# Start offsets of the split activations in four feed-forward stages

## The reference

```
h = rms_norm(x, g)                       # 256 x 1024
gate, up = split(h @ w13)                # 1024 x 5632, D_FF = 2816
x = x + 0.5 * rms_norm(silu(gate) * up @ w2)     # 2816 x 1024
```

## Time and profile before

| what | value |
|---|---|
| device time, 3 runs | 2018.49, 2027.36, 2029.08 us |
| median | 2027.36 us |
| profiled execution, own time | 2015.41 us |
| its span | 2013.2 us |
| granted TensorE clock in it | 0.998 of full speed |
| PE busy | 1977.8 us (98%), 15408 matmuls |
| PEld busy | 1843.3 us (92%) |
| DVE, ACT, POOL busy | 1342.0, 1082.5, 51.9 us |
| HBM read | 353.65 MB, 176 GB/s over the span |

### The profile page before, as it was taken

One profiled execution on the slowest core, in us unless ns is written; L12 is line 12 of the kernel. 1 busy time (PEld: TensorE's weight loads), 2 busy tenths in 40 slices (PEclk: granted clock), 3 DMA queues, 4 the chain that ended last, 5 costly groups with the idle time before them and its releaser, 6 DMA issues.

```text
span 2013.2 us, 37724 instructions
## 1 busy us (share of the span) xinstructions
PE 1977.8 (98%) x15408; PEld 1843.3 (92%) x15408; DVE 1342.0 (67%) x1866; ACT 1082.5 (54%) x1698; POOL 51.9 (3%) x47
## 2 busy tenths in 40 slices
PE   7999999999999999999999999999999999999998
PEld 7989989999899989899988998999899989888997
DVE  6776766787566657866867555655477678756554
ACT  5846555555454454555556444644454565645443
POOL 0021000000000000000100000000000001000000
PEclk9999999999999999999999999999999999999999
DMA  7521455566566647543553655565655535545553
GB/s 274 168 85 66 144 189 168 198 202 199 176 218 194 199 168 232 184 137 128 208 199 137 230 192 196 187 211 190 198 193 184 177 109 189 181 159 168 189 190 123
DMA packets 98729, 359.30 MB, mean 178 GB/s; under 512 B 11192, under 2 KB 11512, under 8 KB 98296
## 3 DMA queue, kind: packets, MB, share of 16 engines
q1 hardware_dynamic: 98560, 356.90, 53.6%
HBM read 353.65 MB, written 1.05 MB: 176 GB/s over the span
## 4 chain that ended last, share of the span: by engine, by line
PE 92%; DVE 4%; ACT 3%; issue 1%; DMA 0%; DVEq 0%; SPq 0%; ACTq 0%
PE ps L1040 17%; PE ps L1042 17%; PE ps L1041 17%; PE ps L1027 8%; PE ps L1114 7%; PE ps L1116 7%; PE ps L1115 7%; PE ps L1196 2%; PE ps L1081 2%; PE ps L1083 2%; PE ps L1082 2%; PE ps L1197 2%; PE ps L1203 2%; DVE wlo L1719 1%; ACT whi L2463 1%
## 5 line engine op out<-in xcount | busy, mean ns | idle before, releaser
L1719 DVE TENSOR_TENSOR wlo<-raw,whi 128x1024 fp32r<-128x1024 f32 x635 | 773.6, 1228 | 458.1 <-ACT whi L2463 456.0
L2463 ACT ACTIVATE whi<-raw 128x1024 fp32r<-128x1024 f32 x635 | 664.5, 1056 | 351.3 <-PE ps L1116 154.4
L1040 PE MATMUL ps<-H,whi 128*128 128x256 f32 x2608 | 732.9, 281 | 2.4 <-DVE wlo L1719 1.6
L1042 PE MATMUL ps<-H,wlo 128*128 128x256 f32 x2608 | 724.6, 278 | 0.0
L1041 PE MATMUL ps<-L,whi 128*128 128x256 f32 x2608 | 724.1, 278 | 0.0
L1040 PEld LDWEIGHTS ps<-H,whi 128*128 128x128 f32 x2608 | 490.0, 188 | 8.3 <-issue 4.0
L1041 PEld LDWEIGHTS ps<-L,whi 128*128 128x128 f32 x2608 | 490.4, 188 | 0.6
L1042 PEld LDWEIGHTS ps<-H,wlo 128*128 128x128 f32 x2608 | 490.3, 188 | 0.0
L1114 PE MATMUL ps<-whi,HH 128*128 128x512 f32 x440 | 171.2, 389 | 0.0
L1115 PE MATMUL ps<-whi,HL 128*128 128x512 f32 x440 | 171.2, 389 | 0.0
L1116 PE MATMUL ps<-wlo,HH 128*128 128x512 f32 x440 | 171.2, 389 | 0.0
(11 more groups left out here) (441 smaller groups left out, 2936.4 us busy)
## 6 DMA issues: line engine op xcount, KB each, us to landing
raw<-in_ws SPq DMA_DIRECT2D x635, 512.0 KB, 3.7
prow<-in_rows SPq DMA_DIRECT2D x11, 512.0 KB, 5.3
row<-in_rows SPq DMA_DIRECT2D x9, 512.0 KB, 6.4
mema<-in_memT SPq DMA_DIRECT2D x4, 512.0 KB, 4.9
mema<-in_mem2T SPq DMA_DIRECT2D x4, 512.0 KB, 6.0
memb<-in_mem2T SPq DMA_DIRECT2D x4, 512.0 KB, 5.7
DT<-in_dec SPq DMA_DIRECT2D x2, 768.0 KB, 6.5
X<-in_x SPq DMA_DIRECT2D x1, 1024.0 KB, 10.9
```

Of the source, the lines that this page charges most:

```text
L1040: e.matmul(o, h, hs[k], start=first and k == 0, stop=False, skip_group_check=True)
L1042: mm = e.matmul(o, lo, hs[k], start=False, stop=last and end, skip_group_check=True)
L1719: e.tensor_tensor(m.wlo[:, n % SPL, :], r, h.bitcast(F32), SUB).then_inc(*c.lo.done(n))
L2463: e.activation(m.whi[:, n % SPL, :], m.raw[:, n % RAW, :], ACT.Copy).then_inc(*c.hi.done(n))
```

## The change

The table `BEGIN` gets other numbers for four stages. `f` goes from (64, 64) to (128, 128), `("a", 0)` to (192, 192), `("b", 0)` to (128, 192), and `("a", 1)` to (192, 128), the first of a pair for `H` and the second for `L`. `("b", 1)` and all others keep theirs. The views still fit in the stores (192 is under the slack of 256). Instructions, their order, their shapes and the waits stay as they are; what differs is the start address in the operands that name `H` or `L` in those stages: written in the junction before, read in `head` and `fin`.

```diff
-BEGIN = {..., "f": (64, 64), ("a", 0): (64, 64), ..., ("b", 0): (64, 64), ("a", 1): (64, 64), ..., ("b", 1): (64, 64)}
+BEGIN = {..., "f": (128, 128), ("a", 0): (192, 192), ..., ("b", 0): (128, 192), ("a", 1): (192, 128), ..., ("b", 1): (64, 64)}
```

More of the change, by code:

```diff
@@ L21 @@
 SPREAD = (16, 40, 58, 82.5)
-BEGIN = {"x0": (64, 64), "mix": (0, 0), "c": (64, 64), "f": (64, 64), ("a", 0): (64, 64), ("m", 0): (64, 64), ("o", 0): (0, 0), ("c", 0): (64, 64), ("b", 0): (64, 64), ("a", 1): (64, 64), ("m", 1): (64, 64), ("o", 1): (0, 0), ("c", 1): (64, 64), ("b", 1): (64, 64)}
+BEGIN = {"x0": (64, 64), "mix": (0, 0), "c": (64, 64), "f": (128, 128), ("a", 0): (192, 192), ("m", 0): (64, 64), ("o", 0): (0, 0), ("c", 0): (64, 64), ("b", 0): (128, 192), ("a", 1): (192, 128), ("m", 1): (64, 64), ("o", 1): (0, 0), ("c", 1): (64, 64), ("b", 1): (64, 64)}
 HIDDEN = {"f": (0, 0), ("a", 0): (0, 0), ("b", 0): (0, 0), ("a", 1): (0, 0), ("b", 1): (0, 0)}
```

## The result

The changed kernel takes 2038.02 us (median of 5 runs, 2035.26 to 2040.09), the kernel before 2027.36 (5 runs, 2018.49 to 2030.23). The ratio reported for these runs is 1.0077, with a 95% interval of 1.0049 to 1.0106; the quotient of the two medians is 1.0053. So slower is clear, and the size is known only as 0.5 to 1%. The forecast was no change, 2026 us; the measured time lies inside the range of 2013 to 2045, but just above the 2037.5 up to which it would have passed for no change. The profiled execution took 2035.79 us over a span of 2033.6, which is 20.4 us more span than the profiled execution of before.

The account below looks back on a forecast made before the run. TensorE's matmul stream was taken to bound the kernel. The profiled 2015.41 us plus 2 x 4.7 = 9.4 us for drawn slow stages gave 2024.8; between that and the median of 2027.36 it took 2026, range 2013 to 2045.

Parts of the forecast that it names:

- What bounds the kernel: Whole kernel: TensorE busy 98% of the span, so a change in matmul pace counts in full; VectorE and ScalarE have slack.
- Two paces at one offset: Feed-forward stages with `H` and `L` at 64: 113.3 or 117.7 ns a matmul, each held for a whole stage.
- Writing `H` and `L` costs nothing: Junctions: writing at other offsets taken as 0, at most 1 us either way; `H` writes outside 573 to 603 ns would refute.
- the floor: Matmuls of the four stages: 113.3 ns, the lowest distance seen; no gain below it expected.
- The bound of 28 us of gain: Four stages, 4224 matmuls: most that could be gained if new offsets removed every bubble, 6.7 ns each, giving 1987 us.
- The forecast case: Four changed stages draw their pace anew, chance one half each: 9.4 us over all fast, 2024.8, taken as 2026; chance 0.35.
- The rival of the slow lock: Four changed stages: reads meet in every matmul at 128 or 192, 120.0 ns, 28.2 us more, 2043.6 us; chance 0.3.
- Its nearest row: Mixers' 512-column matmuls with stationary operand at 64, distance 192: 233.3 ns, 6.6 more than at 0, so 192 read as slow.
- The test I named in advance: `fin` of four stages: if `f` and `("a", 0)` differ and the mixed stages lie between by thirds, offset rules, not draw.
- The sign that I had set for the forecast being wrong: `fin` of the four stages: forecast wrong if all four show a pace not seen in the profile before.
- The rule of the Trainium skill: TensorE has two independent SBUF read ports, so the four stages run at 109.2 ns at every offset; change worth 0.

Follow-up runs that it names:

- the second shifted kernel: Kernel before with `whi` and `wlo` 64 bytes further on, `H` and `L` both at 64, 128, 192, 0, 64 in the five feed-forwards: 2045.26 us, one run.

## Why the prediction was wrong, point by point

*What bounds the kernel* held: 19.2 of the 20.4 us are matmul pace in three of the four stages, with TensorE never idle there and the other engines unchanged.

*Two paces at one offset* held, and with them goes most of the spread of the runs. *Writing `H` and `L` costs nothing* held: its sign, durations of `H` outside 573 to 603 ns, was passed by 1 and 3 ns (572, 606) with the median unchanged at 592. So did the floor: no feed-forward in 14 profiles went under 113.3 ns. The bound of 28 us of gain stayed untouched.

*The forecast case failed in "neither offset ruling it out".* 192 doesn't rule the fast pace out, 128 does. At 128 the stage locks at 118.7 ns, and 128 for one part with 192 for the other locks at 118.9 or 121.1. In place of 2 x 4.7 = 9.4 us for four draws, three stages had a fixed price: against the profiled execution before, in which all four were fast, 5.7 (`f`), 7.9 (`("b", 0)`) and 5.6 us (`("a", 1)`), 19.2 us together, and only `("a", 0)` was left to the draw (it was fast). With the slow share of the draws at 64 taken as 3 of 14, the kernel before pays 3 x 4.7 x 3/14 = 3.0 us in these three stages, and the expected loss is 19.2 - 3.0 = 16.2 us, 0.8% of 2027. The ratio of 1.0077 agrees; the medians lie only 10.7 us apart, and the interval holds both.

*The rival of the slow lock* had the right side and the right kind of effect, a fixed slow pace, at a chance of 0.3. Its price of 28.2 us for four stages came out as 19.2 for three, since the locks cost 5.3, 7.8 and 5.6 ns a matmul and not 6.7. Its working has a slip besides: 233.3 - 226.9 is 6.4 ns, not 6.6 or 6.7, so 27 us. Its nearest row misled me about the place. From 512-column matmuls with the activation stationary at 64 I read that the distance 192 is slow for a moving operand; at 256 columns, 192 behaves as 64, in the pace it can have at least, and the slow places are 0 (120.0) and 128. A row with operands in other roles and another width was no guide to which offset is slow: at 512 columns the distance 0 is the fastest of those seen (226.7 ns), at 256 columns it is the slowest of the multiples of 64 with both parts alike. That the price read there, 6.7 ns, is that of 0 at 256 columns may be luck. The test I named in advance, `f` and `("a", 0)` unlike and the other two between by thirds, half came true: they are unlike, but the mixed stages don't lie between 118.7 and 113.3. They lie at 121.1 and 118.9, so a pair isn't the mean of its parts. The sign that I had set for the forecast being wrong, a new pace in all four stages, was too strict: three had one.

*The rule of the Trainium skill* ("TensorE: Matmul & The Clock Gate", on what happens when a matmul is issued), that loading the next weights takes nothing from the running matmul, isn't borne out here: with the same instructions, the distance between the two operands moved the pace from 113.3 to 120.0 ns. That the two reads get in each other's way is my reading of it; why they should at some distances isn't settled. The runs show which distances, not the mechanism, and I have no model that gives 118.7 for 128, 116.6 for 16 and 32, or the draw at 64.

## What to carry to other kernels

In a kernel bound by matmuls, count the matmuls in windows of equal length in every stage: a pace that differs between stages of the same shape is time that no wait and no idle row shows. Look at the place of the moving operand relative to the stationary one, and try both parts of a split at the same distance. Here, at 256 columns, odd multiples of 64 bytes were at the fast pace in part of the profiles, while 0, 128 and all mixed pairs never were. At 512 columns it was 0 that was fast, so try each shape for itself. Where a pace is drawn, one profile shows one draw, so a change of some tenths of a per cent needs ten runs and more.

## What the runs showed of the hardware

- fp32r matmuls of 128x128 by 256 columns, each with its own weight load, at full clock: 113.3 or 117.8 ns from start to start at distances 64 and 192, 118.7 at 128, 120.0 at 0. At 0 all durations in a stage are alike (283 ns), at 128 they vary from 279 to 285 ns.
- In all profiles a pace, once there, holds through the 960 matmuls of `fin` (108.4 us with every duration at 276 ns in the fast case), though VectorE, ScalarE and the DMAs work beside it all the time.
- For 512 columns the distance counts too, and otherwise. With the activation stationary at 64 and the weights at 0, distance 192, it was 233.3 ns. With the activation stationary and everything at multiples of 256 bytes the pace was 226.7 ns; with the weights moved by 64 bytes under the hidden activations (the second shifted kernel) it was 229.0 in `("b", 0)`, first row, (1299.8 - 1241.4) / 85 / 3, against (1293.6 - 1235.8) / 85 / 3 in the changed kernel, second row:

```profile
L1115 PE MATMUL ps<-whi,HH x86: 388/388/400, 1241.4 to 1299.8; 128*128 128x512 f32 x86
```

```profile
L1114 PE MATMUL ps<-whi,HH x86: 389/389/389, 1235.8 to 1293.6; 128*128 128x512 f32 x86
```
